# First layer's scaled input: DVE makes the full form, ACT the upper form alone

## The reference

```
for i in range(4):                                   # mixers: gMLP, Conformer convolution, MLA, gMLP
    s1, a1, g1, s2, a2, g2 = split(silu(c) @ ada_w[i] + ada_b[i])
    x = LN(ALPHA * x + g1 * mixer_i(x * (1 + a1) + s1))
    x = LN(ALPHA * x + g2 * SwiGLU(x * (1 + a2) + s2))
```

## Time and profile before

| what | value |
|---|---|
| median of three runs | 3134.82 us (3131.73 to 3137.52) |
| profiled execution, its own time | 3137.26 us |
| its span | 3135.5 us |
| TensorE (PE) busy with matmuls | 3019.7 us, 96% |
| VectorE (DVE) busy | 1426.7 us, 46% |
| ScalarE (ACT) busy | 555.7 us, 18% |
| GpSimd (POOL) busy | 1502.1 us, 48% |
| mean granted TensorE clock | 0.989 of full speed |

### The profile page before, as it was taken

How to read it: one execution, slowest core, us unless ns; L and a number is a source line. 1 busy time by engine, 2 the same in 40 slices (tenths; PEclk the granted TensorE clock), 3 DMA queues, 4 the chain that set the end, 5 groups by cost and what they waited for, 6 DMA issues and landing times.

```text
span 3135.5 us, 52792 instructions
## 1 busy us (share of the span) xinstructions
PE 3019.7 (96%) x21984; PEld 2788.6 (89%) x21984; DVE 1426.7 (46%) x2530; ACT 555.7 (18%) x1115; POOL 1502.1 (48%) x889
## 2 busy tenths in 40 slices
PE   6999999999999999999989999999999999999998
PEld 4799999999876699999976688999997999899997
DVE  3153663424654763423566546242364536634233
ACT  2230140000220340000233323000023311400001
POOL 2455445545465345555520045554544464455554
PEclk8999999999999999999999999999999999999999
DMA  6642343232345343424321334333322333222321
GB/s 237 226 121 76 121 169 123 82 121 83 90 117 157 130 173 113 145 91 159 92 61 42 104 125 167 122 132 123 127 68 81 98 89 93 69 84 85 88 82 64
DMA packets 450475, 354.80 MB, mean 113 GB/s; under 512 B 26120, under 2 KB 424832, under 8 KB 437933
## 3 DMA queue, kind: packets, MB, share of 16 engines
q1 hardware_dynamic: 435744, 324.79, 32.8%
q10 hardware_dynamic: 14493, 26.63, 2.8%
HBM read 337.86 MB, written 5.25 MB: 109 GB/s over the span
## 4 chain that ended last, share of the span: by engine, by line
PE 85%; DVE 7%; DVEq 2%; ACT 2%; DMA 1%; issue 1%; SPq 1%; ACTq 0%; POOLq 0%; POOL 0%
PE pb L977 83%; DVE h_lo L2382 1%; DVEq L2333 1%; DVE pb L2351 1%; DMA ada_first<-in_ada_w 1%; DVE part L2332 1%; DVE xa L2358 1%; ACT h_hi L1828 1%; ACT hf L1828 1%; PE pb L1672 0%; PE pb L1086 0%; DVEq L2357 0%; DVE h_lo L2392 0%; DVE hf L2373 0%; DVE xa L2356 0%
## 5 line engine op out<-in xcount | busy, mean ns | idle before, releaser
L884 POOL TENSOR_SCALAR w_hi<-w_raw 128x1024 fp32r<-128x1024 f32 (+2 forms) x416 | 444.0, 1067 | 1347.1 <-DMA w_raw<-in_ffn_w_up 405.1
L887 POOL TENSOR_TENSOR w_lo<-w_raw,w_hi 128x1024 fp32r<-128x1024 f32 (+2 forms) x416 | 987.2, 2373 | 69.0 <-issue 69.0
L977 PE MATMUL pb<-h_hi,w_hi 128*128 128x288 f32 x3584 | 974.8, 297 | 12.2 <-DVE h_lo L2392 7.0
L977 PE MATMUL pb<-h_lo,w_hi 128*128 128x288 f32 x3584 | 968.2, 295 | 0.0
L977 PEld LDWEIGHTS pb<-h_hi,w_hi 128*128 128x128 f32 x3584 | 674.3, 188 | 23.6 <-DVE h_lo L2392 12.0
L977 PEld LDWEIGHTS pb<-h_lo,w_hi 128*128 128x128 f32 x3584 | 675.1, 188 | 0.3
L977 PE MATMUL pb<-a_hi,w_hi 128*128 128x288 f32 x2176 | 592.8, 297 | 4.7 <-DVE a_lo L2199 3.9
L977 PE MATMUL pb<-a_lo,w_hi 128*128 128x288 f32 x2176 | 587.4, 295 | 0.0
L977 PE MATMUL pb<-h_hi,w_lo 128*128 128x288 f32 x3584 | 561.8, 295 | 0.0
L977 PEld LDWEIGHTS pb<-h_hi,w_lo 128*128 128x128 f32 x3584 | 504.9, 188 | 0.7 <-POOL w_lo L887 0.5
L977 PEld LDWEIGHTS pb<-a_hi,w_hi 128*128 128x128 f32 x2176 | 408.5, 188 | 13.2 <-issue 6.9
(11 more groups left out here) (321 smaller groups left out, 2699.6 us busy)
## 6 DMA issues: line engine op xcount, KB each, us to landing
ada_w<-in_ada_w SPq DMA_DIRECT2D x80, 1024.0 KB, 8.1
w_raw<-in_ffn_w_gate SPq DMA_DIRECT2D x88, 512.0 KB, 3.8
w_raw<-in_ffn_w_up SPq DMA_DIRECT2D x88, 512.0 KB, 3.8
w_raw<-in_gmlp_w_in SPq DMA_DIRECT2D x64, 512.0 KB, 4.0
w_raw<-in_ffn_w_down SPq DMA_DIRECT2D x64, 512.0 KB, 3.8
w_raw<-in_gmlp_w_out SPq DMA_DIRECT2D x32, 512.0 KB, 4.4
w_raw<-in_ffn_w_down SPq DMA_DIRECT2D x32, 384.0 KB, 3.3
w_raw<-in_conv_w_pw SPq DMA_DIRECT2D x24, 512.0 KB, 4.0
```

Source lines behind the costliest of these rows:

```text
L884: nc.gpsimd.tensor_scalar(w_hi[:, s, 0:w], w_raw[:, s, 0:w], 1.0, 1.0, ALU.mult, ALU.mult).then_inc(split_hi, 1)
L887: nc.gpsimd.tensor_tensor(w_lo[:, s, 0:w], w_raw[:, s, 0:w], w_hi[:, s, 0:w].bitcast(F32), ALU.subtract).then_inc(split_lo, 1)
L977: return nc.tensor.matmul(out, lhsT, rhs, start=start, stop=stop)
```

## The change

ACT's `apply` for t = 0 writes only `h_hi`, and its wait on `h_ready` is gone for t = 0. DVE gets a new function, `scaled_input(m, h)`, one TENSOR_SCALAR (multiply by `cs`, add `cb`) that writes the full form of one tile's prompt columns. DVE calls it for four tiles before each `first_half(g)`, and for two tiles before `samples(0, p)` and `second_half(p)`, with drains between. The other seven norms are as before.

```
-                        if n >= 2:
+                        if t and n >= 2:
                             act.wait_ge(h_ready, n - 1)
...
-                            for dst in (hf[:, g, i, 0:w], h_hi[:, m, h * HALF:h * HALF + w]):
+                            for dst in ((hf[:, g, i, 0:w],) if t else ()) + (h_hi[:, m, h * HALF:h * HALF + w],):
                                 last = fn(dst, xa[:, m, h * HALF:h * HALF + w], ACT.Identity,
...
+            def scaled_input(m, h):
+                w = HP if h else HALF
+                v.tensor_scalar(hf[:, m // 4, m % 4, 0:w], one(xa, m, slice(h * HALF, h * HALF + w)),
+                                cs[:, 0, m, 0:1], cb[:, 0, m, 0:1], ALU.mult, ALU.add)
...
             for g in range(2):
+                for m in range(4 * g, 4 * g + 4):
+                    scaled_input(m, 0)
+                dve.drain()
                 first_half(g)
             for p in range(4):
+                dve.drain()
+                for m in (2 * p, 2 * p + 1):
+                    scaled_input(m, 1)
                 samples(0, p)
                 second_half(p)
```

## The result

The changed kernel took 3139.67 us in the median of 20 runs (3134.87 to 3147.33) against 3132.39 for the kernel before (20 runs, 3128.36 to 3138.53): a ratio of 1.0024 with an interval of 1.0017 to 1.0030, which is 5.3 to 9.4 us more. The forecast was 3139.9, made of 3134.82 and 5.1 us. That the point was met so closely is partly luck: the kernel before was 2.4 us faster over 20 runs than over three, and the cost, 7.3 us, was about 2 us larger than the 5.1 of the forecast. The two errors cancel.

The account below looks back on a forecast made before the run. TensorE's matmuls bound the kernel (85% of the chain), so vector-engine changes count only where TensorE waits. Its second gap ending 4.1 us later plus 1.0 of clock gives 5.1; with the 3134.82 median, 3139.9 us, range 3131.5 to 3145.

Parts of the forecast that it names:

- DVE is released 2.1 and 4.2 us earlier by ACT: First layer's scaled input: without 16 ACTIVATEs, ACT's upper forms end at 43.24 and 45.3; DVE had waited until 45.35 and 49.50.
- DVE and POOL exclude each other, and a waiting POOL gets in between undrained scalars: Scaled-input stage, SBUF access: first h_lo ends at 49.37, 2.7 us later; TensorE's second gap ends 4.1 us later.
- Rival (a): Scaled-input stage: undrained DVE instructions hold POOL out; +3.5 and clock 2 to 3, so +6.5 us, 3141.3; chance 0.23.
- (b): Scaled-input stage: new TENSOR_SCALARs do not take POOL's ports, only h_lo and sample instructions wait; +1.7 us, 3136.5; chance 0.15.
- (c): Scaled-input stage: DVE always goes first, POOL is pushed into DVE's waits; gains 3.5 us, 3131.3; chance 0.08.
- The second h_lo at 14.0, the end at 24.3: DVE's list beside POOL's: second h_lo ends at 54.98, the four second-half pairs at 65.28, in trace time.
- The length of a scalar: DVE's new TENSOR_SCALARs: 0.37 us at 288 columns, 0.34 at 224; a second-half pair grows from 1.88 to 2.57.
- The clock, 1.0: TensorE after its second gap: wait grows from 1.40 to 2.9 us; half-clock matmuls cost 1.0 us, up to 1.7.
- The rest of the chain passes it on whole: After 61.64 us the chain is matmuls alone, so the 5.1 us reach the end undiminished.
- Rival (d): Behind 61.64 us: the lateness is taken up, for instance at a wait for a transfer; 0 us, 3134.8; chance 0.12.
- The class: Whole kernel's time: 0.73 within 0.2% (6.3 us) of no change, 0.24 slower, 0.03 faster.

Follow-up runs that it names:

- e12: Changed kernel without the 16 scalars, lower forms taken from the unscaled input; one run, no ratio; TensorE restarts 19.98 us after ACT's release (before 20.67, changed 25.79).
- e4: Changed kernel with each TENSOR_SCALAR replaced by a SCALAR_TENSOR_TENSOR, one input from SBUF and the shift from PSUM; ratio to before 1.0011 (1.0002 to 1.0020).
- e8: Changed kernel with POOL's third weight unit held until both first-half h_lo instructions; one run, no ratio; DVE's pairs end 25.83 us after ACT's release (changed 25.30).
- e5: Changed kernel with e4's scalars and the first four statistics instructions moved between DVE's second and third pair; ratio to before 0.9999 (0.9990 to 1.0008).

## Why the prediction was right

The direction, the mechanism and the place were right. The cost was forecast as 5.1 us and measured as 7.3: 1.0 of the difference is in the restart and 0.5 in the clock, and the last 0.7 is between the trace (6.6) and the medians, inside their interval.

- *DVE is released 2.1 and 4.2 us earlier by ACT.* Right, and worth little, as e12 shows.
- *DVE and POOL exclude each other, and a waiting POOL gets in between undrained scalars.* Right: after the release the first h_lo was forecast at 8.41 (49.37 less 40.96) and ended at 8.49. Rival (a), scalars that hold POOL out, gave 5.3; (b), scalars beside POOL, 4.5; (c) 3.7. So all three are out. Rival (b)'s path is what e4 shows for another instruction (4.53). That 8.41 came within 0.1 has some luck in it, for one tie went the other way: scalar 1, which I had ahead of w_lo, came behind it (it took 2.59).
- *The second h_lo at 14.0, the end at 24.3.* Measured 14.64 and 25.30. POOL's fourth w_hi stood at its own transfer until 8.0, a wait that I had not in the list; it and the w_lo behind it then caught scalars 4 and 5 (1.15 and 2.62). 0.5 before the second h_lo is time that the profile puts on nothing.
- *The length of a scalar.* 0.42 and 0.39 where no one waits, not 0.37 and 0.34: the rows of a form with one multiply were too short for multiply and add. A pair took 2.67, not 2.57, and the restart came 5.1 instead of 4.1 later.
- *The clock, 1.0.* It was 1.5: the wait of TensorE was 3.72, longer than the 2.9 I had, and 3.3 us at half clock followed.
- *The rest of the chain passes it on whole.* 6.6 at the transposes and 7.3 in the time agree. Rival (d) is out.
- *The class.* I gave 0.73 to within 0.2%. The ratio 1.0024 lies just outside, its interval (1.0017 to 1.0030) on both sides of that bound. What put it there are the mis-sized terms above: the length of the scalars, the second h_lo and the clock.

## What to carry to other kernels

When work moves to an engine that looks idle, look at which neighbour excludes it in that stretch, and lay the two lists side by side with the trace's own durations; the idle time is not free if the neighbour fills it, and short instructions between a neighbour's long ones are the dearest (e8). When a wait goes, walk on to the next one in the same cycle of buffers: here banks, statistics, a GELU, transfer issues and a clearing stood in one line, and the gain came only when the last of them had moved.

## What the runs showed of the hardware

- Between two undrained TENSOR_SCALARs of DVE a waiting POOL instruction gets its turn, each time: of the first eight, six took 0.87 to 2.62 us instead of 0.42. DVE likewise gets its turn between two of POOL's.
- A SCALAR_TENSOR_TENSOR with one input from SBUF and one from PSUM (a single column, read again for every element) is not held up by POOL: 0.51 for 288 columns and 0.44 for 224, slower alone than the TENSOR_SCALAR's 0.42 and 0.39, and 1.79 against 6.96 for four beside POOL.
- What a wait of TensorE before its second half brought in low clock, as the lateness of the transposes beyond that of the restart: nothing after 0.89, 1.15 and 1.40 us, 1.5 us after 2.27, 3.25, 3.72, 4.28 and 7.64, and 2.4 after 4.77. So the price doesn't simply grow with the wait; it went with how much work then ran at 0.50, 3.3 us after the 3.72 and 5.4 after the 4.77. A wait of 2.41 in e5, at 72.3, was followed by full clock (29 matmuls in the 3.4 us from 72.4), where the 2.27 of e12 was not. After 3.72 the clock was still 1.00 through the wait and 0.50 only from 66.4 on, in the work that followed.
- The same kernel's span behind 174 us differed by 8.7 us from one execution to another, with DVE's rows of the stage before it equal to 0.01 us. 5.5 of these are in TensorE's waits; its clock also stood at 0.50 for 7 us more (41 against 34).
